# Attention stage of a streaming encoder step: in each TensorE step the value products move behind the score unit

## What is computed

```
A:  s = q.k / 8 + bias ;  m = max(max(s), sink) ; p = exp(s - m)
    out = (p / (sum(p) + exp(sink - m))) . v        keys of two tiles
B:  s = q.k / 8 + bias, -inf where not chosen ;  out = softmax(s) . v   all keys up to the tile
y = x + concat(outA * silu(gateA), outB * silu(gateB)) @ w_out
```

## Time and profile before

| | |
|---|---|
| median of three runs | 5192.75 us |
| profiled execution | 5191.41 us, its span 5189.6 us |
| granted TensorE clock, mean over the span | 0.92 |
| TensorE matmul busy | 4365.5 us (84%) |
| TensorE weight load busy | 2717.3 us (52%) |
| VectorE busy | 3466.5 us (67%) |
| ScalarE busy | 3454.7 us (67%) |
| GpSimd busy | 1623.0 us (31%) |

### The profile page before, as it was taken

One profiled execution on the slowest core, in us unless ns is written; L12 is line 12 of the kernel. 1 busy time (PEld: TensorE's weight loads), 2 busy tenths in 40 slices (PEclk: granted clock), 3 DMA queues, 4 the chain that ended last, 5 costly groups with the idle time before them and its releaser, 6 DMA issues. The chain is left out here.

```text
span 5189.6 us, 78325 instructions
## 1 busy us (share of the span) xinstructions
PE 4365.5 (84%) x26505; PEld 2717.3 (52%) x26505; DVE 3466.5 (67%) x6644; ACT 3454.7 (67%) x6887; POOL 1623.0 (31%) x1358
## 2 busy tenths in 40 slices
PE   6767777777687786767689999989999999989999
PEld 3334443434343343433466767767777776754444
DVE  1266788888797898988476766676666668625111
ACT  1578788988787797872478888858787785520100
POOL 1345556667557756777110000000000000000000
PEclk9888888888788898988799999999999999999999
DMA  6211111100010111001521111011010010034423
GB/s 143 66 44 43 37 38 39 34 30 34 30 44 32 37 45 39 33 32 56 157 64 52 43 50 39 27 53 39 25 41 25 27 37 26 12 112 134 112 102 101
DMA packets 201975, 276.98 MB, mean 53 GB/s; under 512 B 50496, under 2 KB 134176, under 8 KB 201056
## 3 DMA queue, kind: packets, MB, share of 16 engines
q1 hardware_dynamic: 198624, 271.81, 16.6%
q10 hardware_dynamic: 2960, 0.17, 0.0%
HBM read 156.73 MB, written 114.16 MB: 52 GB/s over the span
## 5 line engine op out<-in xcount | busy, mean ns | idle before, releaser
L595 PE MATMUL bank<-w,x 128*128 128x512 f32 (+1 forms) x2848 | 1245.9, 593 | 26.3 <-DVE w L940 13.7
L1042 DVE TENSOR_SCALAR_CACHE_REDUCE ties<-score,cand 128x512 int8<-128x512 f32 (+13 forms) x448 | 1110.5, 2479 | 122.3 <-POOL score L916 106.9
L595 PEld LDWEIGHTS bank<-w,x 128*128 128x128 f32 x2848 | 571.3, 204 | 608.2 <-issue 540.1
L806 ACT ACTIVATE act_junk<-score,a_cand,a_sign 128x384 int8<-128x384 f32 (+13 forms) x420 | 879.4, 2094 | 14.0
L1832 DVE CUSTOM_DVE_ANT_0 row<-bank,mask 128x512 f32<-128x512 f32 (+3 forms) x1024 | 622.5, 638 | 384.1 <-PE bank L1571 383.5
L613 PE MATMUL bank<-kiT,qi 128*128 128x512 f32 (+3 forms) x1136 | 394.2, 489 | 414.9 <-DVE kiT L960 211.4
L1538 POOL TENSOR_TENSOR near_bias<-table,mask 128x2048 f32<-128x2048 f32 (+1 forms) x32 | 129.5, 4047 | 1830.6 <-DVE part L1832 1815.1
L1766 ACT ACTIVATE pT<-bank 128x512 f32<-128x512 f32 (+2 forms) x704 | 368.0, 523 | 449.3 <-PE bank L1587 447.3
L1587 PE MATMUL bank<-ident,row 128*128 128x128 f32 x4224 | 607.3, 283 | 52.0 <-DVE pT L1943 43.4
L1668 ACT ACTIVATE row<-row,top 128x1024 f32<-128x1024 f32 (+7 forms) x640 | 632.9, 990 | 3.4 <-DVE top L1845 3.4
L1571 PE MATMUL bank<-kT,qb 64*128 64x256 f32 (+1 forms) x4352 | 608.4, 396 | 7.9 <-DVE part L1832 5.1
(11 more groups left out here) (255 smaller groups left out, 4904.9 us busy)
## 6 DMA issues: line engine op xcount, KB each, us to landing
qk_t<-ring SPq DMA_DIRECT2D x66, 256.0 KB, 2.0
gates<-ring SPq DMA_DIRECT2D x66, 256.0 KB, 2.0
gate<-gates SPq DMA_DIRECT2D x33, 512.0 KB, 3.4
out<-x_in SPq DMA_DIRECT2D x33, 512.0 KB, 2.9
x<-in_x_prompt SPq DMA_DIRECT2D x32, 512.0 KB, 3.8
mixed<-mixT SPq DMA_DIRECT2D x64, 256.0 KB, 2.0
mix_in<-mixed SPq DMA_DIRECT2D x32, 512.0 KB, 4.5
x_in<-in_x_prompt SPq DMA_DIRECT2D x32, 512.0 KB, 3.9
```

The costliest lines, as they stand in the source:

```text
L595: ins = pe.matmul(p_bank[n % 2][:, 0:n1 - n0], held[:, c * P:(c + 1) * P], w[:, c, n0:n1], start=(c == 0), stop=(c == KC - 1))
L806: tick(act.activation(junk, row, ACT.Sign, bias=c, scale=back, accum_out=a_sum[:, :]))
L1042: n = tick(dve.tensor_scalar(ties[:, 0:width], row, c.bitcast(F32), 0.0, ALU.is_ge, ALU.add, accum_out=counts[:, i:i + 1]))
```

## The change

In TensorE's loop over steps, the call of `apply` moves from before the step's score units and gate transposes to behind them. Nothing else differs.

```diff
             for n in range(N_JOBS):
                 for g in range(n_steps(n)):
                     turn(n, g)
-                    if last is not None:
-                        apply(*last)
-                    last = (n, g)
                     for kind, m, j in PLACED[n, g]:
                         if kind == "score":
                             score(m, j)
                         else:
                             turn_gate(m, j)
+                    if last is not None:
+                        apply(*last)
+                    last = (n, g)
             apply(*last)
             turn_gate(TILES - 1, 1)
```

## The result

The changed kernel takes 5152.3 us (median of four runs, 5150.3 to 5163.2) against 5193.2 before: a ratio of 0.9927, 95% interval 0.9911 to 0.9942 (30 to 46 us), or 40.9 us. The profiled execution has a span of 5149.2 us (before 5189.6) at the same mean granted clock of 0.92.

A forecast was written before the change was run, and what follows sets the result against it. TensorE bounds the attention stage (96 to 97% busy); order can touch its waits for VectorE and ScalarE. 54 us less 16 plus 5 gives 43 us off: 5150 us predicted, own range 5125 to 5175, 8 in 10 5112 to 5184.

The forecast's parts named there:

- (1): Attention stage: units come earlier, so VectorE's copy delays transposes less; 38 us off wide jobs, 16 off band jobs.
- The cap by the length of A: A wait for VectorE's copy shrinks by at most the value products moved, 1.02 us in full steps.
- (2): At a tile's edge ScalarE is late next and takes back 40% of 40 us, 16 us.
- (3): Switches between TensorE's groups sum to the same in the new order: 0 us, bounds 98 us either way.
- S to A: TensorE's switch from score unit to value products, not in the trace; taken as 0.33 us.
- Rival B: Switch from score units to value products is dear, 98 us at 0.17 us more; slower, 5205 us; chance 0.06.
- C: More gain: cheaper switch to value products, or ScalarE takes nothing or waits less; 5060 to 5130 us; chance 0.12.
- T and G: A step's transposes and the gate's transposes, in a row, run without any gap.
- (4): Gate steps with a unit, once a tile: three switches instead of four, 32 times 0.15 us, 5 us.
- (5): Waits the move makes, at VectorE's gate product, copies to pT and later units: 0, at most 5 us.
- Rival A: Attention stage: ScalarE's waits rise as VectorE's fall, keeping some 10 us or less; 5183 to 5193 us; chance 0.08.
- Rival D: Step's and gate's transposes, one stretch of 12, lose the full clock; costs 190 us, 5340 us; chance 0.02.

The follow-up runs named there:

- Run 2: Kernel before, with the value products moved behind units and gate only in the 62 steps holding a band unit; 5170.4 us, ratio 0.9951.
- run 4: Changed kernel, but VectorE waits for the value products before it begins its use of a unit; 5264.3 us, ratio 1.0137.
- Runs 5 and 6: ScalarE's late search shortened to 128 columns (wrong output), on the kernel before and on the changed kernel; 5185.6 and 5137.7 us.
- run 9: Changed kernel, but half of the value products stand ahead of the step's units and gates, half behind; 5231.3 us, ratio 1.0075.
- run 1: Kernel before, with only the gate's transposes moved ahead of the value products, score units staying behind them; 5197.9 us, ratio 1.0008.
- run 10: Changed kernel, with ScalarE's exponentials of job 6t+3 no longer begun in band steps, all in job 6t+2; 5115.0 us, ratio 0.9851.
- run 3: Kernel before, with the value products moved behind units and gate everywhere but in the 62 band-unit steps; 5195.0 us, ratio 1.0003.

## Why the prediction was right

5150 was predicted, 5152.3 measured; 43 us forecast, 40.9 found.

(1) *Unit earlier.* Forecast: 38 us off the waits of wide jobs, 16 off those of band jobs, line 1943 down to about 50. Found 37.5, 16.5 and 46.2. The cap by the length of A held: of the two scans' waits, 9.1 and 6.7 us, 8.5 and 5.7 are left. Run 2 finds two thirds of these 54 us in the 62 steps where VectorE has most to do, and in run 4, with the head start alone taken away, the waits are back at 103.5 in sum.

(2) *ScalarE takes back 16.* Its waits rose by 13.6, all in the band jobs. Runs 5 and 6 show that this is time taken. That something would be taken back was reasoned; the 40% was a middle between none and all, and that it came so near is partly luck.

(3) *Switches.* S to A is 0.33 us, the step 3.11: 0. Behind the few score units that end in a 128-column stream the gap is 0.12, before and after, so the excess does follow the length of the stream that ends S, as the prediction had it. Rival B's dear switch did not come, nor C's cheap one. Rival B's time was also added up wrongly in the prediction: 98 us on top of the forecast are 5248, not 5205. (The 576 are the wide units; they stand in 562 steps, so its 98 us are 96.) The Trainium skill states a drain for any change of tiling mode (TensorEngine Tiling (Array Packing), Key Properties). The trace agrees: 0.17 us stands at a change of group (0.33 behind a 256-column score stream), run 9's extra changes add to it, and there is none between T and G, which are alike.

(4) *Gate steps, 5 us.* In sum the forecast holds: over all the stage's loads "issue" is 4.9 us less (402.4 to 397.5), with 32 changes between unlike groups fewer in the trace. But it is no gain of the gate's move alone, as run 1's expectation had it. There the gate waits for VectorE's use of an earlier unit, and nothing is gained. In the changed kernel that wait does not grow (5.8 us against 6.0), as VectorE is earlier too.

(5) *New waits, 0 to 5.* 3.4 us in the row of the score units, 5.5 in all. About right in size, but for a reason that I had not given: run 4 shows some 56 us of such waits which only the head start keeps away. As waits: 54.0 less, 13.6 and 5.5 more leaves 35; with the 4.9 of switches and small rest terms that is the 41.1 us of idle time.

So the mechanism was right, and the sum as well; that it came within 2 us is closer than its terms (2), (4) and (5) were known.

Rival A (ScalarE takes all) failed: ScalarE's waits grew before the band jobs only, and run 10, which relieves just those steps, takes 35 us off them. Rival D (clock) failed for the changed kernel, whose granted clock is 1.00 in the stretches that had it, with G behind T in each tile.

## What to carry to other kernels

In an engine's hand-written order, put first what another engine must pick up, and behind it the work whose result nobody awaits. Price it as a head start: each wait shrinks by at most the work moved, and half of that work may do almost as well. Before moving filler, look also at the wait that it covers where it stands. Then look at the engine that is late next: a single line of ScalarE's plan was worth as much (37 us) as the whole reordering, and the waits by kind of step pointed to it. Where executions differ in granted clock, compare idle times beside the medians: run 3's gain showed only there.

## What had not been expected of the hardware

The clock granted in the first tiles of the stage is not the same for nearly equal kernels: 0.76 in the same 120 us for run 3, 0.83 for run 1, 0.84 for both the kernel before and the changed one, and 0.94 to 1.00 in the 200 us behind it. That was some 15 us in run 3 (21 over the whole stage), as large as what that experiment was to show. What sets it stays open.
